# One chain of 16 RWKV matrices with 32-row blocks in the inverse, and gate products in six lumps, in a two-layer hybrid trunk

## The reference

```python
p = h @ w_in                      # RWKV-7 | mLSTM | branch gates
x += (1+g1) * W_out( sig(gR) * P_R(RWKV7(p_R)) + sig(gM) * P_M(mLSTM(p_M)) )

def rwkv7_recurrence(r, w, k, v, a, b):      # 8 heads of 64
    def step(s, inp):
        r_t, w_t, k_t, v_t, a_t, b_t = inp
        sa = jnp.einsum('bhvk,bhk->bhv', s, a_t)
        s = s * w_t[:, :, None, :] + sa[..., None] * b_t[:, :, None, :] + v_t[..., None] * k_t[:, :, None, :]
        return s, jnp.einsum('bhvk,bhk->bhv', s, r_t)
```

## Time and profile before

| | us |
|---|---|
| timed runs (3) | 1440.77 median, 1438.9 to 1441.27 |
| profiled execution | span 1437.0 (the page gives no time beside it) |
| TensorE busy | 1419.4 |
| VectorE busy | 1048.7 |
| ScalarE busy | 298.9 |
| mixer stretch, layer 0 | 372.71 to 464.69 |
| mixer stretch, layer 1 | 1070.40 to 1162.38 |

### The profile page before, as it was taken

One profiled execution on the slowest core, in us unless ns is written; L12 is line 12 of the kernel. 1 busy time (PEld: TensorE's weight loads), 2 busy tenths in 40 slices (PEclk: granted clock), 3 DMA queues, 4 the chain that ended last, 5 costly groups with the idle time before them and its releaser, 6 DMA issues.

```text
span 1437.0 us, 29272 instructions
## 1 busy us (share of the span) xinstructions
PE 1419.4 (99%) x12848; PEld 1332.5 (93%) x12848; DVE 1048.7 (73%) x1792; ACT 298.9 (21%) x586; POOL 72.2 (5%) x142
## 2 busy tenths in 40 slices
PE   7999999999999999999999999999999999999998
PEld 3999999898988999999999999988898889999998
DVE  5899888787634669987988886787972456756656
ACT  3111102532223031110031110045222311211101
POOL 7100000000000000000000000000000000000000
PEclk9999999999999999999999999999999999999999
DMA  9998876243422657887758876364432247466440
GB/s 348 336 335 302 306 290 195 89 132 104 117 62 90 227 188 260 296 300 292 248 193 266 285 275 235 127 166 132 133 103 61 61 147 263 148 206 205 179 145 30
DMA packets 214046, 283.03 MB, mean 197 GB/s; under 512 B 13288, under 2 KB 177504, under 8 KB 213920
## 3 DMA queue, kind: packets, MB, share of 16 engines
q1 hardware_dynamic: 194976, 211.11, 45.0%
q0 software_dynamic: 17952, 69.21, 13.2%
q10 hardware_dynamic: 992, 0.85, 0.2%
HBM read 280.10 MB, written 1.05 MB: 196 GB/s over the span
## 4 chain that ended last, share of the span: by engine, by line
PE 97%; DMA 1%; SPq 1%; DVE 1%; issue 0%; ACT 0%; ACTq 0%; DVEq 0%
PE ps L1792 96%; DMA arena<-in_ada_w_dram 1%; PE ps L1796 1%; SPq L549 0%; SPq L544 0%; DVE arena L1651 0%; DVE hT L1777 0%; DVE arena L1646 0%; DVE x L1191 0%; ACT xn L680 0%; ACTq L254 0%; SPq L542 0%; SPq L541 0%; DVEq L1776 0%; ACTq L994 0%
## 5 line engine op out<-in xcount | busy, mean ns | idle before, releaser
L1792 PE MATMUL ps<-hT,ring 128*128 128x128 f32 (+2 forms) x2448 | 399.4, 319 | 1.3 <-ACT hT L680 1.3
L1792 PEld LDWEIGHTS ps<-hT,ring 128*128 128x128 f32 (+1 forms) x2448 | 348.1, 190 | 35.5 <-issue 8.6
L1792 PE MATMUL ps<-y_both,arena 128*128 128x128 f32 x2304 | 266.6, 275 | 1.0 <-issue 1.0
L1792 PEld LDWEIGHTS ps<-y_both,arena 128*128 128x128 f32 x2304 | 261.8, 192 | 1.5 <-issue 1.5
L1792 PEld LDWEIGHTS ps<-arena 64*64 64x64 f32 (+1 forms) x3792 | 221.4, 153 | 17.0 <-issue 11.2
L1792 PE MATMUL ps<-arena 64*64 64x64 f32 (+3 forms) x3792 | 235.4, 243 | 1.3
L1792 PE MATMUL ps<-arena,ring 128*128 128x128 f32 (+1 forms) x1312 | 186.5, 294 | 0.0
L1792 PEld LDWEIGHTS ps<-arena,ring 128*128 128x128 f32 x1312 | 171.3, 192 | 6.6
L1018 DVE SCALAR_TENSOR_TENSOR ada_acc<-ada_stage,cond,ada_acc 128x1024 f32<-128x1024 f32 (+1 forms) x119 | 149.0, 1252 | 5.8 <-DMA ada_stage<-in_ada_w_dram 2.2
L1792 PE MATMUL ps<-y_both,ring 128*128 128x128 f32 (+1 forms) x1024 | 150.8, 301 | 0.0
L1792 PEld LDWEIGHTS ps<-y_both,ring 128*128 128x128 f32 x1024 | 138.6, 192 | 6.4
(11 more groups left out here) (306 smaller groups left out, 1371.8 us busy)
## 6 DMA issues: line engine op xcount, KB each, us to landing
ring<-in_ffn_w_in_dram SPq DMA_DIRECT2D x86, 1024.0 KB, 7.8
ada_stage<-in_ada_w_dram POOLq DMA_DIRECT2D x66, 1024.0 KB, 5.9
ring<-in_ffn_w_out_dram SPq DMA_DIRECT2D x44, 1024.0 KB, 6.2
ring<-in_mix_w_in_dram SPq DMA_DIRECT2D x46, 512.0 KB, 5.0
ring<-in_mix_w_in_dram SPq DMA_DIRECT2D x12, 1024.0 KB, 5.7
ring<-in_mix_w_in_dram SPq DMA_DIRECT2D x6, 1536.0 KB, 6.2
ring<-in_mix_w_out_dram SPq DMA_DIRECT2D x8, 1024.0 KB, 5.2
arena<-in_ada_w_dram SPq DMA_DIRECT2D x6, 1024.0 KB, 13.7
```

Of the source, the lines that this page charges most:

```text
L1792: return nc.tensor.matmul(out_, lhsT, rhs, start=start, stop=stop, **kw)
```

## The change

- The two groups become one chain of 16 matrices: every level is done once over all of them, with operations of 512 columns on VectorE and ScalarE.
- The 16-wide and 32-wide levels work on the four 32-row diagonal blocks of each matrix: 64 products of 32x32 by 32 columns for each level (`blocks`). The masks for it are made by "n" (four 32-row blocks) and "o64" (the two off-diagonal blocks of the 64-wide level). The last level makes only the off-diagonal block ("g64", "xo"), and the whole inverse is put together in `xf` by VectorE copies, a ScalarE copy and zeros from GpSimd.
- The masked products for mrb, mak and mrk are separate products ("mrb", "mk") and are placed between the levels.
- The gate calls stand in lumps: 14 at "b", "d", "f" and "h", 10 at "j" and 26 at the end ("tail"), none at "a", "c", "e", "g", "i". The 4 at "num" stay.
- Head norms of the RWKV output are done once over both groups, the y transposes both behind "branch m 1", and PSUM banks, the wait of the third branch load (now "qt") and the mask constants follow.

```diff
-GATE_PLACES = (("num", 4), ("heads", 4), ("masks 0 a", 8), ("masks 0 b", 4), ("inverse 0 p", 2), ("inverse 0 a", 2), ("inverse 0 b", 2),
-       ("inverse 0 c", 2), ("uz 0", 2), ("y 0 a", 5), ("y 0 b", 4), ("y 0 c", 2), ("next", 3),
-       ("masks 1 a", 8), ("masks 1 b", 4), ("inverse 1 p", 2), ("inverse 1 a", 5), ("inverse 1 b", 2),
-       ("inverse 1 c", 4), ("uz 1", 2), ("y 1 a", 5), ("y 1 b", 4), ("y 1 c", 2), ("tail", 14))
+GATE_PLACES = (("num", 4), ("a", 0), ("b", 14), ("c", 0), ("d", 14), ("e", 0), ("f", 14), ("g", 0), ("h", 14),
+       ("i", 0), ("j", 10), ("tail", 26))
...
-sp.wait_ge(*DV.at(l, "qt 1"))
+sp.wait_ge(*DV.at(l, "qt"))
...
+if half:
+    po.wait_ge(*PE.at(l, "num"))
+    po.memset(xf[32:64, :, 0:32], 0.0).then_inc(*PO.step())
+    po.memset(xf[96:128, :, 0:32], 0.0).then_inc(*PO.step(f"xf {l}"))
...
+def copied(label, dst, bank):
+    ac.wait_ge(*PE.at(l, label))
+    act(dst[:, :, :], view(ps[:, bank, :], 16, 32), ACT.Copy, label)
+copied("p2", p2, 2)
+gates("a")
+turned("v", 0, 3)
+copied("p4", n16, 1)
+gates("b")
+turned("v", 1, 2)
+turned("a", 0, 3)
+copied("p8", p2, 1)
...
+copied("g64", p2, 1)
+gates("f")
+ac.wait_ge(*PE.at(l, "xo"))
+act(xf[0:32, :, 32:64], view(ps[0:32, 0, :], 16, 32), ACT.Copy, "xo")
+gates("g")
+for n, bank in ((0, 3), (2, 2)):
+    ac.wait_ge(*PE.at(l, f"uz {n}"))
+    act(uz[:, 4 * n:4 * n + 4, :], quad(bank), ACT.Copy, f"uz {n}")
+gates("h")
...
+dv.wait_ge(*PE.at(l, "n"))
+masked(n16, "n16", 0)
+dv.wait_ge(*DV.last(l))
+flipped("nt16", nt16, n16)
+masked(o32, "o32", 1)
+dv.wait_ge(*DV.at(l, "nt16"))
+free(V.tensor_tensor(xt[:, :, :], nt16[:, :, :], spread[:, :].unsqueeze(1).broadcast_to([P, 16, 32]),
+                     ALU.add), "xt 1")
+dv.wait_ge(*PE.at(l, "mrb"))
+for h in range(2):
+    free(V.tensor_tensor(mrb[:, h::2, :], view(ps[:, 4 + h, :], 8, 64),
+                         mask_t[:, 0, :].unsqueeze(1).broadcast_to([P, 8, 64]), ALU.mult),
+         "mrb" if h else None)
+dv.wait_ge(*AC.at(l, "p2"))
+flipped("p2t", p2t, p2)
+grow("xt 2", 0)
+dv.wait_ge(*AC.at(l, "p4"))
+flipped("p4t", nt16, n16)
+masked_mk(0)
+grow("xt 4", 0)
+masked_mk(1)
+grow("xt 8", 0)
+dv.wait_ge(*DV.last(l))
+flipped("x32", p2t, xt)
+grow("xt 32", 0)
+dv.wait_ge(*DV.last(l))
+flipped("x64", p2t, xt)
+for r in range(4):
+    rows, at = slice(32 * r, 32 * r + 32), 32 * (r % 2)
+    free(V.tensor_copy(xf[rows, :, at:at + 32], xt[rows, :, :]))
+dv.wait_ge(*PE.at(l, "xo"))
+free(V.tensor_copy(xf[64:96, :, 32:64], view(ps[64:96, 0, :], 16, 32)), "xf")
...
+for n, bank in ((1, 1), (3, 0)):
+    dv.wait_ge(*PE.at(l, f"uz {n}"))
+    free(V.tensor_copy(uz[:, 4 * n:4 * n + 4, :], quad(bank)), f"uz {n}")
...
+head_sums(l, y_heads, 16, 64, y_squares, "r")
+head_scaled(l, y_heads, 16, 64, "r")
...
-def batch(label, n, bank, lhsT, rhs, waits, wide=64):
-    for w in waits:
-        pe.wait_ge(*w)
-    for i in range(4 * n, 4 * n + 4):
-        at = i % 4 * wide
-        for c in chunks:
-            dst = ps[c, 3 * n + bank, at:at + wide]
-            last = mm(dst, lhsT[c, i, :], rhs[c, i, :])
-    last.then_inc(*PE.step(f"{label} {g} {n}"))
...
-for n in range(2):
-    batch("p4", n, 0, p2t, p2, [AC.at(l, f"p2 {g} {n}"), DV.at(l, f"p2t {g} {n}")])
-    batch("xt 2", n, 2, p2, xt, [DV.at(l, f"xt 1 {g}"), DV.at(l, f"m_n {g} 2")])
-gates(f"inverse {g} a")
...
+def blocks(label, bank, lhsT, rhs):
+    for i in range(16):
+        for rows in quarter:
+            last = mm(ps[rows, bank, 32 * i:32 * i + 32], lhsT[rows, i, :], rhs[rows, i, :])
+    last.then_inc(*PE.step(label))
+pe.wait_ge(*DV.at(l, "prep 1"))
+turned_heads()
+pe.wait_ge(*DV.at(l, "gates 0"))
+for q, t, h, hh in heads:
+    ar, bt, kt, hats = sets[q // 2]
+    at = 32 * (2 * q + t)
+    for r, rows in enumerate(quarter):
+        last = mm(ps[rows, h, at:at + 32], ar[hh, q % 2, t, 0, rows],
+                  bt[hh, q % 2, t * P + 32 * r:t * P + 32 * r + 32])
+last.then_inc(*PE.step("n"))
+pe.wait_ge(*DV.at(l, "gates 1"))
+for q, t, h, hh in heads:
+    ar, bt, kt, hats = sets[q // 2]
+    at = 32 * (2 * q + t)
+    for c in range(2):
+        last = mm(ps[quarter[2 * c + 1], 2 + h, at:at + 32], ar[hh, q % 2, t, 0, quarter[2 * c + 1]],
+                  bt[hh, q % 2, t * P + 64 * c:t * P + 64 * c + 32])
+last.then_inc(*PE.step("o64"))
+pe.wait_ge(*DV.at(l, "y_m"))
+for q, t, h, hh in heads:
+    ar, bt, kt, hats = sets[q // 2]
+    at = 64 * (2 * q + t)
+    for c in range(2):
+        last = mm(ps[chunks[c], 4 + h, at:at + 64], bt[hh, q % 2, t * P + 64 * c:t * P + 64 * c + 64],
+                  ar[hh, q % 2, t, 1, chunks[c]])
+last.then_inc(*PE.step("mrb"))
...
+pe.wait_ge(*DV.at(l, "nt16"))
+pe.wait_ge(*AC.at(l, "o64"))
+blocks("p2", 2, nt16, n16)
+gates("a")
+turned("v", 0, 3)
+pe.wait_ge(*AC.at(l, "p2"))
+pe.wait_ge(*DV.at(l, "xt 1"))
+pe.wait_ge(*DV.at(l, "o32"))
+blocks("xt 2", 0, p2, xt)
+pe.wait_ge(*DV.at(l, "p2t"))
+blocks("p4", 1, p2t, p2)
+pe.wait_ge(*DV.at(l, "mrb"))
+products_mk(0)
+gates("b")
+turned("v", 1, 2)
+pe.wait_ge(*AC.at(l, "turned v 0"))
+turned("a", 0, 3)
+pe.wait_ge(*AC.at(l, "p4"))
+pe.wait_ge(*DV.at(l, "xt 2"))
+blocks("xt 4", 0, n16, xt)
+pe.wait_ge(*DV.at(l, "p4t"))
+blocks("p8", 1, nt16, n16)
+pe.wait_ge(*DV.at(l, "kr 0"))
+products_mk(1)
+gates("c")
+pe.wait_ge(*AC.at(l, "turned v 1"))
+turned("a", 1, 2)
+pe.wait_ge(*AC.at(l, "turned a 0"))
+turned("b", 0, 3)
+pe.wait_ge(*AC.at(l, "p8"))
+pe.wait_ge(*DV.at(l, "xt 4"))
+blocks("xt 8", 0, p2, xt)
+gates("d")
+pe.wait_ge(*AC.at(l, "turned a 1"))
+turned("b", 1, 2)
+pe.wait_ge(*AC.at(l, "turned b 0"))
+turned("k", 0, 3)
+pe.wait_ge(*DV.at(l, "xt 8"))
+blocks("g32", 1, o32, xt)
+pe.wait_ge(*DV.at(l, "kr 1"))
+for q, t, h, hh in heads:
+    i = 4 * q + 2 * t + h
+    for c in chunks:
+        last = mm(ps[c, 4 + i // 8, 64 * (i % 8):64 * (i % 8) + 64], mk[c, i, 0:64], v_tm[c, q, t, hh])
+last.then_inc(*PE.step("z0"))
+pe.wait_ge(*DV.at(l, "x32"))
+pe.wait_ge(*AC.at(l, "g32"))
+blocks("xt 32", 0, p2t, p2)
+gates("e")
+pe.wait_ge(*AC.at(l, "turned b 1"))
+turned("k", 1, 2)
+pe.wait_ge(*DV.at(l, "xt 32"))
+for i in range(16):
+    for c in range(2):
+        last = mm(ps[quarter[2 * c], 1, 32 * i:32 * i + 32], o64[quarter[2 * c + 1], i, :],
+                  xt[quarter[2 * c + 1], i, :])
+last.then_inc(*PE.step("g64"))
+gates("f")
+pe.wait_ge(*DV.at(l, "x64"))
+pe.wait_ge(*AC.at(l, "g64"))
+for i in range(16):
+    for c in range(2):
+        last = mm(ps[quarter[2 * c], 0, 32 * i:32 * i + 32], p2t[quarter[2 * c], i, :],
+                  p2[quarter[2 * c], i, :])
+last.then_inc(*PE.step("xo"))
+gates("g")
+pe.wait_ge(*PO.at(None, f"xf {l}"))
+pe.wait_ge(*DV.at(l, "xf"))
+pe.wait_ge(*AC.at(l, "xo"))
+for n, bank in enumerate((3, 1, 2, 0)):
+    for i in range(4 * n, 4 * n + 4):
         for c in chunks:
...
+            last = mm(ps[c, bank, i % 4 * P:i % 4 * P + P], xf[c, i, :], az[c, i, :])
+    last.then_inc(*PE.step(f"uz {n}"))
+gates("h")
+pe.wait_ge(*AC.at(l, "uz 2"))
+pe.wait_ge(*DV.at(l, "uz 3"))
...
+gates("i")
+pe.wait_ge(*AC.at(l, "h"))
+pe.wait_ge(*DV.at(l, "gt"))
+chain_step(1)
+pe.wait_ge(*DV.at(l, "qt"))
+for q, t, h, hh in heads:
+    i = 4 * q + 2 * t + h
+    for c in chunks:
+        mm(y_of(q, t, h)[c, :], mrb[c, i, :], uz[c, i, 64:128], start=q == t == 0, skip_group_check=True)
+        mm(y_of(q, t, h)[c, :], mk[c, i, 64:128], v_tm[c, q, t, hh], start=False, skip_group_check=True)
+pe.wait_ge(*DV.at(l, "chain 1"))
+chain_step(2)
+gates("j")
+pe.wait_ge(*DV.at(l, "chain 2"))
+for q, t, h, hh in heads:
+    for c, cc in chunks_of(t, 1, 4):
+        last = mm(y_of(q, t, h)[cc, :], qt[hh, 2 * q + t, cc], state(q, c)[hh, :],
+                  start=False, stop=True, skip_group_check=True)
+last.then_inc(*PE.step("y"))
...
+pe.wait_ge(*DV.at(l, "y"))
 for j in range(4):
     if j >= 2:
         pe.wait_ge(*AC.at(l, f"gates {4 + j}"))
     branch(0, j, y_m, "branch m")
     if j == 1:
+        pe.wait_ge(*DV.at(l, "r normed"))
+        y_turned(0)
         y_turned(1)
```

More of the change, by code:

```diff
@@ L367, in trunk @@
         sw, cum, aa, kk, kp, d_neg = (carve(2, T) for n in range(6))
[L369 to L378, removed]
+        taken[0] = chain
+        mrb = carve(16, 64)
+        o64 = carve(16, 32)
+        mk = carve(16, P)
+        xf = carve(16, 64)
+        small = taken[0]
+        n16, nt16, o32, xt, p2, p2t = (carve(16, 32) for n in range(6))
+        taken[0] = small
+        uz = carve(16, P)
+        h_s = carve(12, 64)
+        qt = view(set_0[:, 1024:2048], 8, P)
+        gt_s = view(set_0[:, 2048:2560], 8, 64)
+        s_s = view(set_0[:, 2560:3072], 8, 64)
+        diag = view(o64.rearrange("p a b -> p (a b)"), 8, 64)
+        y_squares = view(mrb.rearrange("p a b -> p (a b)"), 2, 8, 64)
         ada_first = view(arena[:, 2048:2048 + 6 * 4 * BLOCK], 6, 4, BLOCK)
@@ L920, in _ @@
                 gates("num")
-                gates("heads")
-                for g in range(2):
[L924 to L935, removed]
```

(31 more changed lines are left out.)

351 lines of the change are left out of this document (124 added, 227 removed).

## The result

The changed kernel takes 1463.28 us (median of 4 runs, 1462.49 to 1465.36) where the kernel before, timed beside it, takes 1441.02 (4 runs, 1438.9 to 1441.78). The ratio is 1.016, with a 95% interval of 1.0146 to 1.0175: slower by 22 us, where the prediction said faster by 20. The profiled execution took 1463.56 us, with a span of 1461.8.

What follows compares the result with a forecast made beforehand. TensorE, busy 99% of 1437.0 us, was taken as the bound. Each layer's 91.98 us window would become 59.5 + 14.9 + 4.3 + 2.3 + 0.9 = 81.9, saving 20.2 in two layers: 1421 us, range 1414 to 1435.

Steps and rivals of the forecast that it cites:

- Supply of instructions: Mixer window term: 127 matmuls a packet, 1.14 us each, packets following one another; 0.9 us added a layer.
- rival B: Half the gain lost: blocks at 11 to 15 ns from slow packets or dear shape changes; 1426 to 1438 us, chance 0.22.
- rival C's lesser form: Two packet times for each packet, 18 ns an instruction: just above 1441 us; counted within the slower case's chance 0.10.
- The "Against" of B: Argument against blocks slowed to 11 to 15 ns: the densest row, 96 instructions in 1.91 us, shows no gap.
- over 1.9 us: Failure sign: groups of 128 32x32 block instructions, expected at 1.0 to 1.1 us plus latency, taking longer than this.
- kept, added and shape terms: One layer's mixer window: products kept 59.5 us, new products 14.9, 25 changes between tile shapes 4.3.
- predicted 82.3: Forecast length of each layer's mixer window by the later ends; the prediction's own sum was 81.9 us.
- other waits: TensorE waiting for VectorE and ScalarE at xt 2, g64, uz, chain 1 and the local y; 2.3 us a layer.
- the 1460 us of that rival: Slower case using the skill page's 25 ns floor: 30 us for 1216 instructions, about 1460 us; slower case's chance 0.10.
- "short gaps" list: Expected sign: short gaps ahead of uz, chain 1 and the local y, none ahead of branch r.
- 3.8 us "of launch and end": Difference between profiled span 1437.0 and timed median 1440.77, added around the kernel to turn 1416.8 into 1420.6 us.
- Changes of shape: TensorE switching tile shapes in the mixer window: at most 0.17 us each, 25 counted after the edit, 4.3 us a layer.

Runs made afterwards that it cites:

- the last kernel of the study: Changed kernel with gate products spread over 16 places, more of them early, and gate-weight transfers split and paced, the first waiting for "n": 1424.59 us, ratio 0.9895 to before.

## Why the prediction was wrong

**The step that failed** is "Supply of instructions". It read 1.14 us a packet from the queue's busy time and let packets "come one behind another", 0.9 us a layer. The packets don't follow one another: their starts are 3.5 us apart when TensorE has nothing left, which their busy share can't show. In the DMA view one starts at 385.0 to 385.5, its first matmul at 387.63, the next packet at 388.5 to 389.0: 2.1 to 2.6 us from start to work, of which the transfer is 1.1, and about 1 us more until the next moves. The text held the right thought in rival B, "a request, then the transfer", and in rival C's lesser form, "two packet times for each packet, 18 ns", and priced neither from a row. The "Against" of B, that 96 instructions in 1.91 us show no gap, is no evidence: 96 is less than one packet.

**The clock was left out.** The prediction has no term and no rival for it; the earlier trace rows showed it full, in a kernel whose TensorE is hardly ever idle there. Stops in the middle of the mixer are not only lost time, they can take the clock with them. Its own signs of being wrong pointed elsewhere: "over 1.9 us" for 128 blocks was meant for slow blocks, and the 1.93 us seen come at half clock, 1.29 at full.

**With these two the sum comes near the measured time, the clock's share being a bound.** For layer 0 the kept, added and shape terms are 59.5 + 14.9 + 4.3 = 78.7, 79.1 by the ends used here. Issue idle is 12.2 (predicted 0.9), other waits 1.3 (predicted 2.3). Half clock costs at most half of the busy time in its stretches, (10.94 + 3.28 + 3.41) / 2 = 8.8. Together 101.4, measured 101.5: the 19.2 us missing from the predicted 82.3 are 11.3 of supply and up to 8.8 of clock, less 1.0 of waits over-counted. In layer 1 it is 79.1 + 13.5 of issue + 1.9 of waits + at most 21.6 / 2 = 10.8 of clock, 105.3, measured 104.8. The close fit is in part luck. The gate products do lose half (8.00 against 6.31 us, with 3.4 us of it at half clock), but 128 blocks lose only a third (1.93 against 1.29), so 8.8 is too much; and each stop hides the last product's own length, some 0.2 us, which no term has. The terms of work find better support in the last kernel of the study: its 84.2 us at full clock less 2.9 of idle are 81.3, against 79.1, with ten more lumps.

**Right:** 8.3 ns for a 32-row matmul on four tiles. The Trainium skill ("TensorE: Matmul & The Clock Gate", Part 1) says that start to start never falls below about 25 ns; the trace shows 209 starts in 1.8 us, so for the engine the rule doesn't hold, and for one tile of four (34 ns) the trace agrees. That the 1460 us of that rival come near the 1463 measured is chance: the blocks did not run at 25 ns, the packets held them up. Right too: 14128 matmuls; g64 waits 0.20 us (0.16 predicted); uz waits 0.84 (0.86), though for VectorE's last copy into `xf`, not for the ScalarE copy from which the figure was worked out; nothing is late ahead of branch r, and the time behind the window is unchanged. The local y waited 0.3 and 0.9 us (0.68); the waits of xt 2 (0.25) and chain 1 (0.39) don't show. TensorE is busy 97%, not 99%: the "short gaps" list lacked the ones that counted. Two small readings were off and change nothing: 3.8 us "of launch and end" mixes a median with one run (the profiled run of the kernel after is 1.8 us above its span), and the 27.9 ns of its sums for 128 columns are 27.2 in its row, 0.1 us.

**Changes of shape** at 0.17 us were not too cheap: the last kernel has ten more lumps in its window than the kernel after, so some twenty more changes, and its 81.3 us are 2.2 above the 79.1 of the sum. That is 0.11 us for each, an estimate as good as the 79.1.

**The packet's size and the stops.** The runs show stops after each 128 matmuls and an early one, one packet into dense work. The Trainium skill ("Advanced Engine Details and Errata", ISA Cache) speaks of cache lines of 16 KB for 256 instructions, and of only 2 of them, but also gives TensorE 128 KB, which would be eight. The 256 agree with the stops; that TensorE starves about one packet after it begins to run dense (155 matmuls, at 376.7 us) fits two and not eight, though no run here counts them.

**The change itself** was sound, and its lumps spoiled it: gate products are most of the work in the window that uses a packet slowly, 0.43 us for two matmuls and their two weight loads. Placed between the rounds they make most packets last 3.5 us; gathered at every second place they leave packets of 1.1 us.

## What to carry to other kernels

Divide the stretch by the packet: behind the packet at hand, any 128 matmuls in a row that take TensorE less than some 3.5 us (27 ns each) outrun the supply, and a faster form then buys little, and may cost the clock. Mix dense small products with long ones so that every packet lasts that long, rather than keep each kind together to save changes of shape; here a change cost 0.11 to 0.17 us and a stop 0.3 to 4.5. Break up large transfers that start in such a stretch. In a profile look for "issue" ahead of the middle of a group of like instructions, at equal distances: the page's share of the instruction queue (0.5% here in both kernels) doesn't give it away.

## What the runs showed of the hardware

- When TensorE starves, with the DMA engines otherwise idle, a packet of 256 of its instructions lets it resume every 3.4 to 3.8 us in most cases (up to 4.1 in layer 1): 27 to 30 ns a matmul, the same for 32-row products at half clock and 64-row products at full clock.
- A packet that falls into a 1 MB transfer of weights comes later: the same two stops are 3.90 and 4.32 us with it and 2.46 and 2.37 without, and one of 2.44 us became 1.07 when the transfer was split. Over all runs the stops are up to 4.5 us with such a transfer and at most 2.5 without.
- One idle of 4.2 us in each layer brought 3.4 and 6.8 us at the granted clock 0.50, beginning inside the idle. While 32-row products starved, it stayed at 0.50 for 13.7 and 17.1 us; while 64-row products on four tiles starved at the same pace, with stops of 1.25 to 1.64 us, it never fell. Yet the last half clock of layer 0 in the kernel after (at 428.94) follows stops of only 0.62, 0.20 and 0.66 us. What decides between these was not tried and stays open, as does what part of the 3.5 us is request and what is take-over.
